# One decoder trunk, two MoE layers: first gate chunks loaded in parts, and other orders and engines for the layer norm and the routing ahead of the experts

## Chip, cores and metric

One core of a Trainium2 chip runs the whole program. The metric is the time of one execution in device microseconds; the median of three runs is given. The profile is one further execution.

## The reference

256 tokens of width 1024 go through two layers. Each layer is a mixer (HGRN2 in layer 0, differential attention in layer 1), a layer norm of `alpha * x + mix`, a mixture of 16 experts, and a layer norm of `alpha * x + ffn`. What matters here is the routing and the experts:

```python
probs = softmax(xt @ router_w); sel = probs + router_b
gscore = top_k(sel.reshape(-1, 4, 4), 2)[0].sum(-1)     # 4 groups of 4 experts
gbest = argmax(gscore)
_, idx = top_k(where(in_group(gbest), sel, -inf), 2)    # two experts of that group
gates = probs[idx] / sum(probs[idx])
h = silu(xt @ w_gate[e]) * (xt @ w_up[e]); y = (h * comb) @ w_down[e]
```

Everything is float32. The expert weights are 6 MB for each expert, 96 MB for a layer.

## The kernel before

**Projections.** The weights of the mixer come in pieces of 512 rows by 512 columns (`PIECES`, 36 in all). For each piece ScalarE writes a rounded copy (`high`), VectorE the rest (`low`), and TensorE (`piece`) makes three products: rounded weights with rounded activations, rounded weights with the rest of the activations, rest of the weights with rounded activations. Within each product it runs over two token tiles `j`. The last piece of a layer's output projection is number 19 in layer 0 and 35 in layer 1, names `(AO1, 1)` and `(BO1, 1)`. VectorE then adds the residual per token tile and takes moments (`residual_projections`): for the second column half both residuals first, then both moments.

**From the layer norm to the experts** (`layer_norm`, `route` on VectorE; `turned_sums`, `root`, `second_parts`, `normalise_for_experts` on ScalarE; `moe` on TensorE). TensorE transposes x of tile 0 and tile 1 into four PSUM banks (L1968). ScalarE copies all four to `xT` (L856), TensorE multiplies them with the router in two parts (L1978), and VectorE (tile 0, L1224) and ScalarE (tile 1, L1071) copy those out for a folding matmul (L1984). The layer norm itself is folded in later, from mean and root. VectorE aggregates the moments (L1219), adds epsilon (L1221), ScalarE takes the logarithm and the exponential of minus a half (L861, L863), VectorE sharpens the root with a Newton step (L1206 to L1208), computes the shift (L1232), and signals `ln_stat`. On that signal ScalarE starts to write the normalised x to `xn` in four quarters (L847), with the router's exponential between (L1075), and VectorE computes logits (L1505, L1510), the exponentials' sum, `sel` (L1520), then the best group: all 4 x 4 differences inside each group, compared with a margin, summed to the number of experts that beat each one (`lost`), the sum of the two that lose to at most one, the same comparisons between groups (L1527 to L1541), and the mask `both` (L1543). `step` makes VectorE wait for the instruction it has just issued. TensorE counts the ranks from `both` (L1993 to L1997), VectorE makes slots (L1551) and a pick matrix (L1457), and TensorE gathers the first pair's tokens from `xn` (L2027). In between TensorE multiplies zeros (`nothing`, L1797): 4 of 512 and 33 of 256 columns ahead of the ranks, 8 behind. Its own instructions run in order.

**Experts.** The experts run in 8 pairs (e, e + 8): gate and up (`into_hidden`, L2057), down (L2071), with adding the previous pair's outputs (L2019) and gathering for later pairs (L2038) between. A pair's weights are 12 chunks of 1 MB: `chunk_of(matrix, part, e)`. The even pairs use 12 slots of a ring, the odd pairs separate places for gate and up (`spare`, `late`, in the trace "weights" and "tail"). SyncE issues all loads in a fixed order; each is issued when TensorE has read what it overwrites (`chunk_read`). Ahead of the stage it has loaded the first pair and, except for one up chunk and parts that the ring needs, the second. Its first load within the stage overwrites gate part 0 of the first pair with that of the third; it waits for the end of that part's matmuls:

```python
load_step(layer, p, p % 2, NEXT_GATES[0:1])
sp.wait_ge(xe_ps, GATHERS * layer + 1)
sp.wait_ge(xr_ready, 2 * layer + 2)
load_chunk(layer, 1, 1, UP, 1, 0)
order = NEXT_GATES[1:] + NEXT_UPS + DOWNS
```

**GpSimd** weighs pick matrices (L760, L767) and, beside the first pairs, applies the layer norm to x in place (`affine`: L744, L748) and scales it (L777).

## Time and profile before

| | us |
|---|---|
| median of 3 runs | 709.13 (708.81 to 710.08) |
| the profiled execution | 710.35 |
| its span in the trace | 708.5 |
| TensorE busy | 692.6 (98%) |
| VectorE busy | 288.6 (41%) |
| ScalarE busy | 231.8 (33%) |
| GpSimd busy | 105.7 (15%) |

The span runs from the first to the last instruction of the trace; 1.85 us of the execution lie outside. "Busy" counts all instructions alike: for TensorE also the multiplications of zeros. The DMA moved 347 GB/s over the span, and up to 423 in single slices of it.

### The profile page before, as it was taken

Reading aid. Unit: us, or ns where it says so; the run is one execution under the profiler, and the core shown is the slowest. Engines: PE = TensorE matmul, PEld = TensorE weight load, DVE = VectorE, ACT = ScalarE, POOL = GpSimd, SP = SyncE. Lnnn points to the kernel's source line nnn. Section 1 sums busy time; section 2 is a strip of 40 time slices with the busy share of each in tenths; the row PEclk is TensorE's granted clock in tenths of the full one; section 3 lists DMA queues with packets and bytes.
Section 4 is the critical chain, followed back from the end, with each engine's and each line's share of the span. In section 5 each row is a group of like instructions: output and inputs, shape, how many; then the busy total and the mean of one; then the engine's idle time right before and its main releaser. Section 6 shows DMA issues by size and latency. Waiting matters only on the chain.

```text
span 708.5 us, 13562 instructions
## 1 busy us (share of the span) xinstructions
PE 692.6 (98%) x5542; PEld 413.0 (58%) x5543; DVE 288.6 (41%) x540; ACT 231.8 (33%) x434; POOL 105.7 (15%) x69
## 2 busy tenths in 40 slices
PE   9999999999999999999999999999999999999994
PEld 7989888864235335335379987886423533533532
DVE  5589956583011112112067676668301111211205
ACT  4466457161111112012064566626111111201202
POOL 3015100019300000000213200001930000000023
PEclk9999999999999999999999999999999999999998
DMA  8999334889999999999999743488999999999992
GB/s 319 297 385 359 141 118 179 319 334 389 420 421 422 421 423 422 422 421 422 416 386 390 268 169 119 179 315 338 386 420 420 422 422 422 422 421 422 422 420 83
DMA packets 51447, 246.16 MB, mean 347 GB/s; under 512 B 6265, under 2 KB 6610, under 8 KB 26834
## 3 DMA queue, kind: packets, MB, share of 16 engines
q1 hardware_dynamic: 51410, 245.65, 86.7%
q8 instruction: 25, 0.41, 0.2%
q14 instruction: 12, 0.10, 0.0%
HBM read 244.58 MB, written 1.05 MB: 347 GB/s over the span
## 4 chain that ended last, share of the span: by engine, by line
PE 87%; DMA 8%; DVE 1%; ACT 1%; issue 1%; SPq 0%; POOL 0%; POOLq 0%; DVEq 0%; ACTq 0%
PE ps L2057 27%; PE ps L1847 15%; PE ps L2071 14%; PE ps L1842 13%; DMA tail<-in_moe_w_up 8%; PE ps L2019 4%; PE ps L2038 3%; PE ps L1797 2%; PE ps L1775 1%; PE ps L2027 1%; PE ps L2108 1%; DMA x_sb<-in_x 1%; ACT xT L856 1%; DVE stats L1664 1%; PE ps L1882 1%
## 5 line engine op out<-in xcount | busy, mean ns | idle before, releaser
L2057 PE MATMUL ps<-weights,scratch 128*32 128x512 f32 (+1 forms) x1536 | 167.8, 592 | 0.0
L2057 PEld LDWEIGHTS ps<-weights,scratch 128*32 128x32 f32 x1536 | 50.0, 110 | 113.8 <-issue 113.8
L2071 PE MATMUL ps<-weights,scratch 128*32 128x512 f32 (+1 forms) x1024 | 113.6, 594 | 0.0
L1187 DVE TENSOR_TENSOR ring_lo<-weights,w_hi 128x2048 fp32r<-128x2048 f32 x36 | 83.1, 2326 | 14.7 <-ACT w_hi L812 14.5
L1640 DVE TENSOR_TENSOR scratch<-ps,early 128x512 f32<-128x512 f32 x16 | 11.1, 692 | 183.9 <-PE ps L2057 183.9
L812 ACT ACTIVATE w_hi<-weights 128x2048 fp32r<-128x2048 f32 x35 | 66.6, 1915 | 25.6 <-PE ps L1847 15.6
L2071 PEld LDWEIGHTS ps<-weights,scratch 128*32 128x32 f32 x1024 | 31.5, 110 | 70.3 <-issue 70.3
L1652 DVE SCALAR_TENSOR_TENSOR rounded<-ps,gslot,rounded 128x512 fp32r<-128x512 f32 x32 | 24.0, 751 | 92.1 <-ACT rounded L1057 92.1
L2057 PE MATMUL ps<-tail,scratch 128*32 128x512 f32 (+1 forms) x512 | 56.8, 592 | 2.0 <-DMA tail<-in_moe_w_up 2.0
L1057 ACT ACTIVATE rounded<-ps,gslot 128x512 fp32r<-128x512 f32 x32 | 22.0, 688 | 88.9 <-PE ps L2071 88.9
L760 POOL TENSOR_TENSOR early<-rounded,gate_of 128x256 f32<-128x256 f32 x14 | 8.6, 616 | 280.8 <-PE ps L2126 279.9
L1022 ACT ACTIVATE scratch<-ps,ln_col 128x256 f32<-128x256 f32 (+1 forms) x40 | 19.3, 540 | 89.9 <-PE ps L2038 84.6
L1040 ACT ACTIVATE early<-ps 128x512 f32<-128x512 f32 x16 | 9.6, 597 | 95.1 <-PE ps L2057 95.1
L2057 PEld LDWEIGHTS ps<-tail,scratch 128*32 128x32 f32 x512 | 16.5, 110 | 40.8 <-issue 40.8
L2019 PE MATMUL ps<-rounded,early_r 128*128 128x512 f32 x128 | 35.9, 410 | 0.0
L1842 PE MATMUL ps<-x_lo,w_hi 128*128 128x256 f32 x256 | 33.8, 285 | 0.0
L748 POOL TENSOR_TENSOR x_sb<-x_sb,scratch 128x2048 f32<-128x2048 f32 x6 | 29.5, 4919 | 26.6 <-DVE scratch L1192 26.2
L1842 PE MATMUL ps<-x_hi,ring_lo 128*128 128x256 f32 x256 | 33.4, 283 | 0.0
L1623 DVE TENSOR_SCALAR scratch<-ps,ln_col 128x256 f32<-128x256 f32 (+1 forms) x40 | 18.7, 512 | 33.4 <-PE ps L2038 33.0
L2038 PE MATMUL ps<-rounded 128*128 128x256 f32 x128 | 32.2, 290 | 0.0
L767 POOL TENSOR_TENSOR early<-rounded,gate 128x256 f32<-128x256 f32 x2 | 5.5, 2740 | 178.1 <-DVE scratch L1623 178.1
L1842 PEld LDWEIGHTS ps<-x_hi,ring_lo 128*128 128x128 f32 x256 | 31.9, 192 | 0.2 <-DVE ring_lo L1187 0.2
(278 smaller groups left out, 973.4 us busy)
## 6 DMA issues: line engine op xcount, KB each, us to landing
weights<-in_moe_w_gate SPq DMA_DIRECT2D x64, 1024.0 KB, 15.4
weights<-in_moe_w_down SPq DMA_DIRECT2D x64, 1024.0 KB, 14.0
weights<-in_moe_w_up SPq DMA_DIRECT2D x32, 1024.0 KB, 15.0
tail<-in_moe_w_up SPq DMA_DIRECT2D x32, 1024.0 KB, 20.4
weights<-in_a_w_in SPq DMA_DIRECT2D x15, 1024.0 KB, 12.8
weights<-in_kv_w SPq DMA_DIRECT2D x8, 1024.0 KB, 15.3
weights<-in_a_w_out SPq DMA_DIRECT2D x4, 1024.0 KB, 14.6
weights<-in_b_w_q SPq DMA_DIRECT2D x4, 1024.0 KB, 15.1
```

The lines of the kernel that those rows point to most:

```text
L748: last = pool.tensor_tensor(x[:, :, :], x[:, :, :], ln_gb[:, j, :].unsqueeze(1).to_broadcast([P, TT, D]), op)
L812: nc.scalar.activation(w_hi[:, i % HI, :, :].rearrange("p k n -> p (k n)"), ring[:, piece_slot(i), :, :].rearrange("p k n -> p (k n)"), AC ...
L1022: last = nc.scalar.activation(xe[:, k, cols], ps[:, bank, j * width:(j + 1) * width], ACT.Identity, scale=ln_col(2 * layer, 0, k), bias=ln ...
L1057: nc.scalar.activation(ys_hi[:, part * COLS:(part + 1) * COLS], ps[:, bank, :], ACT.Copy, scale=gslot[:, 0:1]).then_inc(ys_act, 1)
L1187: V.tensor_tensor(low_part(i), ring[:, piece_slot(i), :, :], w_hi[:, i % HI, :, :].bitcast(F32), ALU.subtract).then_inc(lo_ready, 1)
L1652: V.scalar_tensor_tensor(ys_lo[:, cols], ps[:, bank, :], gslot[:, 0:1], ys_hi[:, cols].bitcast(F32), ALU.mult, ALU.subtract).then_inc(ys_d ...
L1842: last = mm(ps[:, bank, c * T:(c + 1) * T], w[:, k, first:first + P], xs[:, HALF_K * part + k, :], start=opens and c == 0 and k == 0, stop ...
L1847: last = mm(ps[:, bank, :], xs[:, HALF_K * part + k, j * P:(j + 1) * P], w[:, k, :], start=opens and k == 0, stop=closes and k == HALF_K - ...
L2019: last = mm(ps[:, 2 * t + j, :], put[:, t * P:(t + 1) * P], part[:, j * COLS:(j + 1) * COLS], start=False, stop=True, skip_group_check=True)
L2038: last = mm(ps[:, banks[j // 2], first:first + 4 * SLOTS], part[:, t, k * P:(k + 1) * P], pick[:, t, :, :].rearrange("p e s -> p (e s)"), ...
L2057: last = mm(ps[rows, bank, :], own[:, HALF_K * part + k, rows], w, start=part == 0 and k == 0, stop=part == 1 and k == HALF_K - 1)
L2071: last = mm(ps[rows, bank, :], hT[:, 2 * part + k, rows], w, start=part == 0 and k == 0, stop=part == 1 and k == 1)
```

## The change

1. **Gate chunks in parts.** The loads that overwrite the first pair's gate part 0 are cut by rows k: k=0 and k=1 are each issued when TensorE has read that k, the last two when it has read the whole part. The short ones are counted on a semaphore `rows_in`, for which SyncE waits before the next gate part.
2. **Last piece by token tile.** TensorE makes all three products of tile 0 before those of tile 1, and waits for the low weights at the start of the piece. VectorE takes residual and moments of tile 0, then of tile 1.
3. **The fourth xT copy** goes from ScalarE to VectorE.
4. **Root.** ScalarE takes the logarithm from the aggregated variance with epsilon as its bias. VectorE halves the variance meanwhile, and has the shift before the root is sharpened; both are then finished by one operation each. This serves all four layer norms.
5. **Groups.** The best group is found by the maximum of the six pair sums of each group; the comparisons inside groups, which the mask needs, run between, with waits only where a result is used. The normalising sum `m2` is taken behind the pick matrix.
6. **A quarter of the rows.** The last of the four quarters of `xn` (tile 1, columns 512 to 1023) goes from ScalarE to GpSimd, on `ln_stat`.
7. 25 zero matmuls in place of 33 ahead of the ranks. Some semaphores are merged.

```diff
+            def load_first_gates(layer):
+                half = ins["moe_w_gate"].shape[2] // 2
+                for k, rows in enumerate((slice(0, 1), slice(1, 2), slice(2, 4))):
+                    if rows.stop < HALF_K:
+                        sp.wait_ge(gate_rows, PAIRS * layer + k + 1)
+                    else:
+                        sp.wait_ge(*chunk_read(PAIRS * layer + 1, GATE, 0))
+                    for e in range(2):
+                        c = chunk_of(GATE, 0, e)
+                        w = ins["moe_w_gate"][layer, 2 + PAIRS * e, 0:half, :].rearrange("(p k) n -> p k n", p=P)
+                        arrived = rows_in if rows.stop < HALF_K else arrive[chunk_slot(layer, c)]
+                        sp.dma_start(chunk_place(layer, 0, c)[:, rows, :], w[:, rows, :]).then_inc(arrived, 16)
...
-                        load_step(layer, p, p % 2, NEXT_GATES[0:1])
+                        load_first_gates(layer)
                         sp.wait_ge(xe_ps, GATHERS * layer + 1)
                         sp.wait_ge(xr_ready, 2 * layer + 2)
                         load_chunk(layer, 1, 1, UP, 1, 0)
+                        sp.wait_ge(rows_in, 64 * (layer + 1))
...
+                pool.wait_ge(ln_stat, 2 * layer + 1)
+                pool.tensor_scalar(xn[:, 1, COLS:D].rearrange("p (k n) -> p k n", k=HALF_K),
+                                   x[:, 1, COLS:D].rearrange("p (n k) -> p k n", k=HALF_K), mv[:, 1, 0:1], rs[:, 2, 1:2],
+                                   ALU.subtract, ALU.mult).then_inc(x_done[1], 1)
...
+            def root_of_variance(i):
+                act.wait_ge(var_ready, i + 1)
+                nc.scalar.activation(rs[:, 1, 0:TT].unsqueeze(2), mv[:, :, 1:2], ACT.Ln, bias=eps[:, 0:1]
+                                     ).then_inc(ln_step, 1)
...
-                step(last)
-                V.tensor_scalar(rs[:, 0, 0:TT].unsqueeze(2), mv[:, :, 1:2], LN_EPS, None, ALU.add).then_inc(var_ready, 1)
+                last.then_inc(var_ready, 1)
+                dve.wait_ge(var_ready, rt_call + 1)
+                step(V.tensor_scalar(rs[:, 0, 0:TT].unsqueeze(2), mv[:, :, 1:2], LN_EPS, -0.5, ALU.add, ALU.mult))
                 if i % 2 == 0:
+                    dve.wait_ge(z_ps, 4 * (i // 2) + 4)
+                    V.tensor_copy(xT[:, HALF_K:KT, P:T], ps[:, 3, :].rearrange("p (k t) -> p k t", k=HALF_K)
+                                  ).then_inc(z_dve, 1)
...
-                step(rstd(rt_call, ln_values))
-                V.scalar_tensor_tensor(rs[:, 4, 0:TT].unsqueeze(2), mv[:, :, 0:1], -1.0, rs[:, 2, 0:TT].unsqueeze(2),
-                                       ALU.mult, ALU.mult).then_inc(ln_stat, 1)
+                dve.wait_ge(root_ready, rt_call + 1)
+                for t in range(TT):
+                    V.scalar_tensor_tensor(t3[:, t:t + 1], first[:, t:t + 1], half_var[:, t:t + 1], first[:, t:t + 1],
+                                           ALU.mult, ALU.mult)
+                step(V.scalar_tensor_tensor(shift.unsqueeze(2), mv[:, :, 0:1], -1.0, first.unsqueeze(2), ALU.mult, ALU.mult))
+                V.scalar_tensor_tensor(y, t3, 1.5, first, ALU.add, ALU.mult)
+                V.scalar_tensor_tensor(shift, t3, 1.5, shift, ALU.add, ALU.mult).then_inc(ln_stat, 1)
...
+                V.tensor_tensor(two_of[:, :, 0:2], four[:, :, 0:4:2], four[:, :, 1:4:2], ALU.add)
+                sums_done = mark(V.tensor_tensor(two_of[:, :, 2:6].rearrange("p g (a b) -> p g a b", a=2), ...))
+                apart = mark(V.tensor_tensor(versus[:, :, :, :], *others(four, NG, 4), ALU.subtract))
+                dve.wait_ge(dve_step, sums_done)
+                best = mark(V.reduce_max(gs, two_of, axis=AX.X))
+                dve.wait_ge(dve_step, apart)
+                won = mark(V.tensor_tensor(versus, versus, margin, ALU.is_gt))
+                dve.wait_ge(dve_step, best)
+                step(V.tensor_tensor(of_groups, *others(gs.rearrange("p (t g) -> p t g", t=TT), TT, GROUPS), ALU.subtract))
+                ahead = mark(V.tensor_tensor(of_groups, of_groups, margin, ALU.is_gt))
+                dve.wait_ge(dve_step, won)
+                V.reduce_sum(lost.rearrange("p (g e) -> p g e", e=4), versus[:, :, :, :], axis=AX.X)
+                dve.wait_ge(dve_step, ahead)
+                step(V.reduce_sum(beaten.rearrange("p (t g) -> p t g", t=TT), of_groups, axis=AX.X))
...
+                if (n, part) in ((AO1, 1), (BO1, 1)):
+                    pe.wait_ge(lo_ready, i + 1)
+                    for j, (number, (w, xs)), k in itertools.product(range(2), enumerate(products), range(HALF_K)):
+                        last = mm(ps[:, 4 + 2 * (n % 2) + j, :], xs[:, HALF_K * part + k, j * P:(j + 1) * P], w[:, k, :],
+                                  start=False, stop=number == 2 and k == HALF_K - 1, skip_group_check=True)
...
-                for _ in range(33):
+                for _ in range(25):
                     nothing(BANK_C, COLS // 2)
...
+                            if matrix == GATE and part == 0 and k < 2 and not odd:
+                                last.then_inc(gate_rows, 1)
```

`mark` signals `dve_step` like `step` but does not wait. The margin operand is broadcast over the groups.

## Rows read from the trace of the kernel before

**Rows 1.** Waits of TensorE: us, times, longest; then a row of its timeline.
```profile
PE ps L2057 <- DMA tail<-in_moe_w_up: 2.0, 2, 1.0
...
681.22 3.21 PE L2057 MATMUL ps<-tail,scratch 128*32 x28 [1.04 <-DMA tail<-in_moe_w_up]
```

**Rows 2.** Windows: start:end, then busy us by engine, granted clock, DMA share, GB/s.
```profile
156.00:162.00 6.00, 6.00 (x60) 1.89 (x56) 5.79 (x18) 2.37 (x2) 4.85 (x2) 1.00 0.33 87
492.00:498.00 6.00, 5.99 (x58) 1.93 (x60) 5.65 (x13) 2.98 (x2) 4.25 (x2) 1.00 0.27 68
340.00:345.00 5.00, 4.04 (x44) 1.05 (x40) 0.00 (x0) 0.60 (x1) 0.00 (x0) 1.00 1.01 419
```

**Rows 3.** Timeline of SyncE: DMA issues ahead of the second pair, layer 0.
```profile
159.25 0.80 SPq L533 DMA_DIRECT2D weights<-in_moe_w_gate  x2
```

**Rows 4.** Chain of work that ended last: gate and up of the first pair.
```profile
155.55 13.94 PE ps L2057 x128
```

**Rows 5.** Timeline of TensorE in layer 0: matmuls of zeros and the gather.
```profile
145.88 4.63 PE L1797 MATMUL ps<-zeros 128*128 128x512 bf16 x37
...
151.72 3.81 PE L2027 MATMUL ps<-rounded,weights 128*128 128x128 f32 x32
```

**Rows 6.** Timeline of VectorE from the last residual to the slots, layer 0.
```profile
142.10 0.69 DVE L1254 SCALAR_TENSOR_TENSOR x_sb<-x_sb,ps 128x512 f32<-128x512 f32 x1 [0.22 <-PE ps L1847]
142.71 1.28 DVE L1258 BATCH_NORM_STATS2 stats<-x_sb 128x6 f32<-128x512 f32 x2
144.02 0.28 DVE L1219 BATCH_NORM_AGGREGATE mv<-stats 128x2 f32<-128x12 f32 x2
144.34 0.17 DVE L1221 TENSOR_SCALAR rs<-mv 128x2 f32<-128x2 f32 x1
...
145.12 0.16 DVE L1206 SCALAR_TENSOR_TENSOR rs<-rs 128x2 f32<-128x2 f32 x1 [0.21 <-ACT rs L863]
...
145.70 0.16 DVE L1232 SCALAR_TENSOR_TENSOR rs<-mv,rs 128x2 f32<-128x2 f32 x1
145.98 0.38 DVE L1505 SCALAR_TENSOR_TENSOR rt<-router_sums,rs 128x16 f32<-128x16 f32 x2
...
148.15 0.29 DVE L1527 TENSOR_TENSOR versus<-rt 128x128 f32<-128x128 f32 x1
...
150.25 0.19 DVE L1543 SCALAR_TENSOR_TENSOR both<-rt,rg 128x32 bf16<-128x32 f32 x1
...
150.92 0.19 DVE L1551 SCALAR_TENSOR_TENSOR slot<-ps,both 128x32 f32<-128x32 f32 x1
```

**Rows 7.** Timeline, layer 1: low weights, then weight loads of the last piece.
```profile
468.48 4.49 DVE L1187 TENSOR_TENSOR ring_lo<-weights,w_hi 128x2048 fp32r<-128x2048 f32 x2
...
472.86 2.23 PEld L1847 LDWEIGHTS ps<-w_hi,rounded 128*128 128x128 f32 x10
```

**Rows 8.** Timeline of ScalarE in layer 0: xT copies and the last normalisations.
```profile
142.70 2.06 ACT L856 ACTIVATE xT<-ps 128x512 f32<-128x512 f32 x4 [12.71 <-PE ps L1968]
...
147.39 3.70 ACT L847 ACTIVATE weights<-x_sb,rs 128x512 f32<-128x512 f32 x3
```

**Rows 9.** Groups by line and shape: a VectorE copy of 512 elements from PSUM.
```profile
L1192 DVE COPY scratch<-ps 128x512 f32<-128x512 f32 x4 | 2.8, 688 | 7.0 <-PE ps L1842 7.0
```

**Rows 10.** Timeline rows of GpSimd and VectorE where both work at once.
```profile
63.39 1.62 POOL L733 TENSOR_TENSOR scratch<-scratch 128x512 f32<-128x512 f32 x1
...
63.78 1.77 DVE L1338 TENSOR_TENSOR scratch<-scratch 128x512 f32<-128x512 f32 x1
...
159.88 7.56 POOL L744 TENSOR_SCALAR x_sb<-x_sb,mv,rs 128x1024 f32<-128x1024 f32 x2
...
176.86 5.38 POOL L777 TENSOR_SCALAR x_sb<-x_sb 128x2048 f32<-128x2048 f32 x1
...
160.04 1.07 DVE L1478 COPY slot_of<-slot 128x16 f32<-128x16 f32 x1
...
161.09 0.16 DVE L1480 TENSOR_TENSOR rt<-rt,rg 128x16 f32<-128x16 f32 x1
```

More of the change, by code:

```diff
@@ L851, in turned_sums @@
             def turned_sums(layer):
-                for n in range(4):
+                for n in range(3):
                     act.wait_ge(z_ps, 4 * layer + n + 1)
@@ L1079, in _ @@
             turned_sums(0)
-            root(2, ln_values)
+            root_of_variance(2)
             second_parts(0)
@@ L1084, in _ @@
             normalise_for_experts(0, 0, 1)
-            for half in range(2):
-                normalise_for_experts(0, 1, half)
+            normalise_for_experts(0, 1, 0)
             moe(0)
-            root(3, ln_values)
+            root_of_variance(3)
             normalise(1)
@@ L1168, in _ @@
             normalise_for_experts(2, 0, 1)
-            for half in range(2):
-                normalise_for_experts(2, 1, half)
+            normalise_for_experts(2, 1, 0)
             moe(1)
-            root(7, ln_values)
+            root_of_variance(7)
             normalise_last()
@@ L1270, in residual_projections @@
                     dve.wait_ge(proj_ready, 2 * n0 + 2 + t + 1)
-                    add_residual(t, 1, ps[:, 6 + t, :])
-                for t in range(TT):
-                    moments(t, 1, added[0] - 1 + t)
-            V.memset(zeros16[:, :], 0.0).then_inc(zeros_ready, 1)
+                    residual(t, 1, ps[:, 6 + t, :])
+            V.memset(zeros16[:, :], 0.0).then_inc(consts_dve, 1)
+            V.memset(eps[:, :], LN_EPS)
             dve.wait_ge(consts_ready, 1)
-            V.tensor_copy(ident_r[:, :], ident[:, :]).then_inc(ident_ready, 1)
+            V.tensor_copy(ident_r[:, :], ident[:, :]).then_inc(consts_dve, 1)
             for half, bank in enumerate((1, 3)):
@@ L1496, in te @@
                     return ap.rearrange("p (t e) -> p t e", t=TT)
-                lg, ex, sel, lost, best2, pm = (rt[:, i, :] for i in range(6))
+                lg, ex, sel, lost, _, pm = (rt[:, i, :] for i in range(6))
                 m2 = rg[:, 0, 0:TT]
@@ L1525, in route @@
                 four = sel.rearrange("p (g e) -> p g e", e=4)
-                other, this = (four.unsqueeze(axis).to_broadcast([P, NG, 4, 4]) for axis in (2, 3))
-                step(V.tensor_tensor(versus[:, :, :, :], other, this, ALU.subtract))
-                step(V.tensor_tensor(versus[:, :, :, :], versus[:, :, :, :],
-                                     margin[:, :, :].unsqueeze(1).to_broadcast([P, NG, 4, 4]), ALU.is_gt))
-                step(V.reduce_sum(lost.rearrange("p (g e) -> p g e", e=4), versus[:, :, :, :], axis=AX.X))
@@ L1531, in route @@
-                step(V.scalar_tensor_tensor(best2, lost, 1.5, sel, ALU.is_lt, ALU.mult))
-                gs = rg[:, 7, 0:NG]
-                step(V.reduce_sum(gs, best2.rearrange("p (g e) -> p g e", e=4), axis=AX.X))
-                sums = gs.rearrange("p (t g) -> p t g", t=TT)
-                other, this = (sums.unsqueeze(axis).to_broadcast([P, TT, GROUPS, GROUPS]) for axis in (2, 3))
-                step(V.tensor_tensor(versus[:, 0:TT, :, :], other, this, ALU.subtract))
-                step(V.tensor_tensor(versus[:, 0:TT, :, :], versus[:, 0:TT, :, :],
-                                     margin[:, :, :].unsqueeze(1).to_broadcast([P, TT, GROUPS, GROUPS]), ALU.is_gt))
@@ L1540, in route, with others @@
-                beaten = rg[:, 8, 0:NG]
-                step(V.reduce_sum(beaten.rearrange("p (t g) -> p t g", t=TT), versus[:, 0:TT, :, :], axis=AX.X))
+                two_of = rt[:, 6:8, :].rearrange("p a n -> p (a n)")[:, 0:6 * NG].rearrange("p (g n) -> p g n", n=6)
+                gs, beaten = rg[:, 7, 0:NG], rg[:, 8, 0:NG]
+                of_groups = rg[:, 9, :].rearrange("p (t a b) -> p t a b", t=TT, a=GROUPS)
+                def others(ap, n, size):
+                    return [ap.unsqueeze(axis).to_broadcast([P, n, size, size]) for axis in (2, 3)]
@@ L1819, in piece @@
                     pe.wait_ge(x_hi_dve, 2 * call + part + 1)
-                for number, (w, xs) in enumerate(((hi, his), (hi, los), (lo, his))):
+                products = ((hi, his), (hi, los), (lo, his))
+                if (n, part) in ((AO1, 1), (BO1, 1)):
[3 more added lines that the diff above has]
+                                  start=False, stop=number == 2 and k == HALF_K - 1, skip_group_check=True)
+                        if number == 2 and k == HALF_K - 1:
+                            last.then_inc(proj_ready, 1)
+                    return
+                for number, (w, xs) in enumerate(products):
                     if number == 1 and first_of_half:
```

50 lines of the change are left out of this document (34 added, 16 removed).

## The prediction, made before the changed kernel ran

> **What bounds the kernel now.** I read the waits first. In each of the two expert stages, TensorE, which is busy nearly all the time, stops once for a transfer, for the last pair's up weights: 2.0 us in two stops, the only ones of the whole trace for a weight transfer, 1.04 of it at 681.22 [rows 1] and 0.96 in the 5 us from 340 [rows 2]. The windows then show why the transfer is late although it was asked for long before. Through the stage the DMA moves about 420 GB/s with nothing to spare; but at the stage's beginning there is a hole. From 156 to 162 us it moves 87 GB/s, from 492 to 498 us 68 GB/s [rows 2]. Against 419 that is 6 x (1 - 87/419) = 4.75 us and 6 x (1 - 68/419) = 5.0 us of empty queue. The queue is empty because the buffers are full: its next transfer overwrites the first gate chunks, and SyncE issues it at 159.25 [rows 3], once the first pair has read all of gate part 0 (it began at 155.55, a quarter of 13.9 us [rows 4]). So DMA and TensorE are balanced, and the stream starts late by a wait on TensorE.
>
> The second thing that bounds the kernel is the stretch ahead of the experts, where TensorE is "busy" with matmuls of zeros. The timeline shows 37 of them from 145.88 to 150.51, and eight more up to the gather at 151.72 [rows 5]. The work that counts there is a chain on VectorE [rows 6]: residual (142.10), moments (142.71), variance (144.34), root, shift (145.70), logits (145.98), groups (148.15 to 150.25), slots (150.92), pick. What is cut from this chain comes off the kernel, in both layers, if the weights keep up.
>
> **The change, part by part.** Times are those of layer 0; layer 1 repeats them, 336.6 us later.
>
> *Gate chunks in parts.* Rows of k=0 are asked for after a quarter of the 3.5 us read of part 0 [rows 4], k=1 after half, the rest as before. The first request moves from 159.25 to about 156.6, 2.6 us ahead of where it stands relative to TensorE. One half MB takes 1.25 us at 420 GB/s, and a quarter of the read is 0.87 us, so the parts follow one another without a new hole. What is queued ahead of the hole ends at 156, the window's left edge, so there is room for it. I take 0.15 to 0.3 us off for shorter rows in 2 of the 96 MB, and are left with 2.3 us of lead. The transfers wanted at the end need 0.96 and 1.04; both stops go: **2.0 us**. The remaining lead is not worth anything, since TensorE has no other wait for it. SyncE issues six DMAs where it issued two, 0.4 us each [rows 3], and then waits for the four short ones to land, about 159; the next thing queued behind is gate part 1, which waits until 162 anyway. Cost nothing; without that cover, at most some tenths of the lead.
>
> *The last piece by token tile.* The same 24 matmuls; tile 0's sums close 2.7 us earlier, tile 1's at the same time. Residual, then moments of tile 0 move into VectorE's idle time; of the two moments behind 142.10 one is left, so aggregation starts at 142.10 + 0.69 + 0.03 + 0.69 + 0.03 = 143.54 in place of 144.02 [rows 6]. The transposes start when the piece ends, and tile 1's wait for the residual that ends at 142.79; both are unchanged. In layer 1 the piece must now have its low weights at its start: these are ready at 468.48 + 4.49 = 472.97, and TensorE's first load is at 472.86 [rows 7], so with 0.05 us for the signal it starts 0.16 us later: **-0.16 us** once.
>
> *Fourth xT copy to VectorE.* ScalarE's four copies end at 142.70 + 2.06 = 144.76 [rows 8]. VectorE is free at 143.82 (aggregation), does the halved variance, and copies 144.06 to 144.75, by the 0.69 us of a PSUM copy of that size [rows 9]. So the router's second half is not earlier. But ScalarE takes the logarithm at about 144.13, behind three copies and with no VectorE step before it. The root is there at 144.6.
>
> *Root and shift.* VectorE, busy with xT and then lgT until about 144.87, runs two tiny products, the shift, then two closing operations. Instructions that need no wait between them start 0.1 us apart (two aggregations in 0.28 us), those with one 0.20 apart (145.12, then four to 145.86) [rows 6]: 0.08 + 0.08 + 0.19 + 0.08 + 0.16 = 0.59, so the shift is out at 145.46 in place of 145.86. **0.40 us.** The second half's logits come at about 146.0 by the unchanged router path, just in time.
>
> *Groups.* From 148.15 to 150.25 eight operations wait each for the one before [rows 6]: 2.10 us. After: nine, two of 128 elements kept apart by others. I lay them out with start-to-start of duration less 0.08 where nothing is waited for and duration plus 0.03 where it is. Starts: sums 0 and 0.09, differences 0.20, maximum 0.41, comparison 0.53, group differences 0.74, comparison 0.965, lost 1.075, beaten 1.285, both 1.50. **0.60 us.** The sum m2 leaves the way from ranks to slots, which started at 150.92 behind it; by the matmuls around them the ranks were there some 0.1 us before, an estimate: **0.08 us**. Eight fewer zero matmuls take 8 x 256 of 10,496 columns, 0.9 of 4.63 us [rows 5], off a queue that ended at 150.51, so it ends at about 149.6, just behind the masks at 149.44: a tie, which the hold below, if it comes, turns into idle time.
>
> *A quarter of the rows on GpSimd.* ScalarE's normalisation ended at 151.09 [rows 8], and would now end by 149.6. GpSimd's part has an unseen price: by the 3.78 us of one 1024-wide operation of the same form [rows 10] it is between 1.9 and 3.8 us; taking 2.62 ns an element from the 5.38 us of 2048 with a constant, and the remaining 1.1 us as fixed, 512 elements cost 2.4. It starts at 145.6 and has until 150.5. Its own time is hidden in every case. Its cost is what it does to VectorE, on whose chain everything above was saved. At 63.78 a two-input VectorE operation of a width that takes 0.7 us (as at 142.10) took 1.77, ending 0.5 us after the GpSimd operation of 63.39 to 65.01. But at 159.88 a GpSimd operation of exactly the new form began, and only the VectorE copy at 160.04 was held, for 0.9 us; the two-input one at 161.09 ran in its usual 0.16 although GpSimd worked until 167.44 [rows 10]. So this form holds VectorE for the first 1.0 us of its run, or, if that goes with the width, for 0.5 us. It would start within 0.02 us of the first logit operation, and is likely to get in between the two, where a hold falls wholly on the chain; if it gets in later, most of the hold ends before the next two-input operation 0.7 us on. The bounds are 0 and 1.05 us per layer; I take 0.5, that of half the width.
>
> The Trainium skill speaks against this part: by its page "SBUF — State Buffer", section "Who interferes with whom", a VectorE instruction with two SBUF inputs and a GpSimd instruction that reads SBUF exclude each other, and the later one waits for the whole of the other. The rows of 63.39 agree; the row of 161.09 does not. By the page the sum would be that of rival 3 below; by the rows it is the one I give.
>
> *The other layer norms.* Between the layers the step ahead of the logarithm (0.2 us) goes and the chain behind it is about as long: **+0.2 us**. At the end VectorE has two copies to make meanwhile, and two more waits: **-0.08 us**.
>
> **Sum.** 2.0 + 0.2 - 0.16 - 0.08 = 1.96, and per layer 0.40 + 0.60 + 0.08 - 0.5 = 0.58, twice 1.16: 3.1 us. The profiled execution took 710.35 us, 1.85 outside its span of 708.5; the median of the runs is 709.13. I take the 3.1 from the median: 706.0 (the profiled time would go to 707.2).
>
> **Rivals.** (1) *No hold at all* on VectorE's two-input operations, as at 161.09: 1.96 + 2.16 = 4.1 us, 705.0. For it: only a copy was seen held. Against: the hold at 63.78. 25%. (2) *The full hold of the first 1.05 us*: 1.96 + 0.06 = 2.0, 707.1. 15%. (3) *The exclusive lock*: the second logit operation is held for all 2.4 us of GpSimd's work. For it: 63.78. Against: 161.09. Per layer 1.08 - 2.4 = -1.3, sum 1.96 - 2.64 = -0.7, 709.8, no change. 10%. (4) *Slower*: the same lock with GpSimd's operation at the upper price, 3.8 us, since it reads with a stride of four; per layer -2.7, sum -3.4, 712.5. It decides from a hold of 2.06 us per layer, and is beyond 0.2% from 2.8. 5%. (5) *The hole is not filled*, because the short rows move slowly or the wait for them blocks SyncE: the stops stay, 3.1 - 2.0 = 1.1, 708.0. 8%. My forecast, a hold of 0.25 to 0.8 us: 34%, by itself 705.3 to 706.6.
>
> The range takes in the forecast and rivals 1, 2 and 5 with 0.6 us for the spread of the runs: 704.4 to 708.3. What a measurement of this kernel can tell from no change is 0.2%, 1.4 us. Faster by more: forecast, 1, 2, and part of 5: 0.78. Within: 3, most of 5: 0.15. Slower: 4 and what I have not thought of: 0.07.
>
> **What the profile after would show.** Right: no wait of TensorE for the up weights; more than 200 GB/s in the six microseconds behind the first gate matmul; the groups in 1.5 us; the gather at about 151.2 in layer 0. A logit or maximum operation of 0.6 us or more beside GpSimd's start shows the hold. Wrong: a VectorE operation of 2 us there (rivals 3, 4); a wait for a transfer that stays (5); or a lower clock of TensorE, which idles up to 0.6 us before the ranks; the stop of 0.96 us left it at 1.00 [rows 2], so I price that at nothing.

## Result: 0.25% slower at first, no different the second time

| | median | lowest to highest | runs |
|---|---|---|---|
| before | 708.83 us | 708.54 to 710.15 | 20 |
| changed kernel | 711.0 us | 707.67 to 713.77 | 20 |

The ratio is 1.0025, 95% interval 1.0013 to 1.0037. Three us faster was forecast. What stands out is the spread: the kernel before repeats itself within some tenths but for single runs near 710.1, the changed one's times are spread over 6 us. Its profiled execution took 713.31 us (span 711.4), the one of before 710.35 (708.5). Both are executions with a slow beginning: at 7.4 us two matmuls of 512 columns took TensorE 1.97 us, where the profiles of experiments e1, e8 and e11 below have 1.07, and from there on everything stands 1.6 to 1.8 us later (tile 1's residual at 142.10 and 142.13, in e8 at 140.28). The two can be compared with each other, but their totals cannot be compared with those of the other profiles. Why the beginning is slow in some executions is open; the rows of the granted clock say 1.00 there in all of them.

The chain of work that ended last in the changed kernel, from the experts of layer 0 to those of layer 1 (start, length, what):

```profile
154.71 13.94 PE ps L2114 x128
...
315.50 1.91 SPq L535
317.45 26.05 DMA tail<-in_moe_w_up
343.74 3.64 PE ps L2114 x32
...
361.21 1.08 PE ps L1842 x19
362.29 2.87 issue
365.15 4.08 PE ps L1842 x41
369.23 1.75 PE ps L1820 x16
```

Cut both kernels at the same marks and compare. Up to the experts: 154.71 against 155.55 [rows 4], 0.84 us saved. From there to the transposes of layer 1's input: 369.23 - 154.71 = 214.52 against 365.42 - 155.55 = 209.87, **4.65 lost**. To the experts of layer 1 (494.90 against 492.15): 125.67 against 126.73, 1.06 saved. To the end: 216.50 against 216.35. Sum +2.9, the difference of the spans. What was changed ahead of the experts gained a little in both layers. The loss lies in the stretch from the experts to the next layer's input, at its end, where only the root of the layer norm was changed.

Two of TensorE's waits in the changed kernel (what for: us in total, times, longest):

```profile
PE ps L1842 <- issue: 2.9, 1, 2.9
PE ps L2114 <- DMA tail<-in_moe_w_up: 2.1, 2, 1.0
```

The first is new: after 19 of the 60 matmuls of zeros that keep TensorE busy between the layers it stops for 2.87 us, and no engine, semaphore or transfer of the program is what it waits for. The second is the wait that was to go, unchanged [rows 1]. VectorE had its part ready meanwhile (start, length):

```profile
363.80 1.53 DVE L1283 TENSOR_SCALAR x_sb<-ps,mv,rs 128x512 f32<-128x512 f32 x2
```

This operation began at 364.56 in the kernel before, and the transposes 0.86 us behind it. Here they could have begun at 364.66 and began at 369.23. The windows (start and end, length, busy time of TensorE, its weight loads, VectorE, ScalarE and GpSimd, then the granted clock, the DMA's share and GB/s) say why it is more than 2.87:

```profile
156.00:162.00 6.00, 6.00 (x60) 1.89 (x56) 5.90 (x17) 1.68 (x3) 5.44 (x2) 1.00 0.74 216
492.00:498.00 6.00, 5.99 (x58) 3.74 (x61) 5.55 (x22) 4.59 (x6) 1.21 (x1) 1.00 0.76 300
...
366.00:367.00 1.00, 1.00 (x12) 1.00 (x10) 0.00 (x0) 0.00 (x0) 0.00 (x0) 0.50 1.07 391
367.00:369.00 2.00, 2.00 (x23) 2.00 (x21) 0.00 (x0) 0.00 (x0) 0.00 (x0) 0.54 1.08 391
369.00:372.00 3.00, 3.00 (x32) 2.93 (x29) 1.85 (x4) 2.07 (x5) 0.00 (x0) 1.00 1.03 382
```

Behind the stop TensorE runs at 0.50 of its clock (1.2 of 2.4 GHz) for most of 3 us: 41 matmuls of zeros took 4.08 us, where the second profile of the same kernel (e11 below) has 41 of them in 2.45 at clock 1.00. That is another 1.6 us. The first two rows answer to [rows 2]: more is moved in the hole of the stream than before (216 for 87 GB/s, 300 for 68).

The routing went nearly as foreseen. VectorE and GpSimd, layer 0:

```profile
142.13 0.69 DVE L1291 SCALAR_TENSOR_TENSOR x_sb<-x_sb,ps 128x512 f32<-128x512 f32 x1 [1.31 <-PE ps L1869]
...
145.43 0.15 DVE L1268 SCALAR_TENSOR_TENSOR rs<-rs 128x2 f32<-128x2 f32 x1
145.70 0.38 DVE L1541 SCALAR_TENSOR_TENSOR rt<-router_sums,rs 128x16 f32<-128x16 f32 x2
...
146.75 0.36 DVE L1550 TENSOR_TENSOR rt<-rt,rg 128x32 f32<-128x32 f32 x1
...
148.04 0.18 DVE L1569 TENSOR_TENSOR rt<-rt 128x16 f32<-128x16 f32 x1
...
149.51 0.19 DVE L1588 SCALAR_TENSOR_TENSOR both<-rt,rg 128x32 bf16<-128x32 f32 x1
```

```profile
145.69 2.69 POOL L791 TENSOR_SCALAR weights<-x_sb,mv,rs 128x512 f32<-128x512 f32 x1 [66.62 <-DVE rs L1268]
```

From the residual to the end of the shift it is 145.58 - 142.13 = 3.45 us, 0.31 less than the 3.76 before (0.40 forecast). The groups take 149.51 - 148.04 = 1.47 us (1.50 forecast, 2.10 before), GpSimd's quarter 2.69 (2.4 forecast), and beside it VectorE loses 0.17 us, at L1550, which takes 0.36 us here and 0.19 in e1.

### The profile page after: what moved, and what is told of

Its sections match the earlier page's. It is cut to its first block, busy times and chain, and to the rows that moved or that the text cites. A ratio compares the mean times of both kernels' runs of the same rounds, so it can differ in the third digit from the quotient of the medians.

```text
span 711.4 us, 13551 instructions
## 1 busy us (share of the span) xinstructions
PE 692.4 (97%) x5526; PEld 413.2 (58%) x5527; DVE 289.6 (41%) x549; ACT 228.9 (32%) x430; POOL 110.8 (16%) x71
## 3 DMA queue, kind: packets, MB, share of 16 engines
HBM read 244.58 MB, written 1.05 MB: 345 GB/s over the span
## 4 chain that ended last, share of the span: by engine, by line
PE 86%; DMA 8%; DVE 3%; issue 1%; ACT 1%; SPq 1%; POOL 0%; POOLq 0%; DVEq 0%; ACTq 0%
PE ps L2114 27%; PE ps L2130 14%; PE ps L1901 13%; PE ps L1896 13%; DMA tail<-in_moe_w_up 7%; PE ps L2076 4%; PE ps L2095 3%; PE ps L1869 2%; PE ps L1820 1%; PE ps L1842 1%; PE ps L2084 1%; PE ps L2167 1%; DMA x_sb<-in_x 1%; PE ps L1936 1%; SPq L535 1%
## 5 line engine op out<-in xcount | busy, mean ns | idle before, releaser
L1896 PEld LDWEIGHTS ps<-x_lo,w_hi 128*128 128x128 f32 x256 | 31.8, 192 | 0.1
```

Source lines behind the costliest of these rows:

```text
L1896: last = mm(ps[:, bank, c * T:(c + 1) * T], w[:, k, first:first + P], xs[:, HALF_K * part + k, :], start=opens and c == 0 and k == 0, stop ...
```

## Experiments

All were timed in five rounds beside the kernel before (medians 708.85, 708.84 and 708.74 in the three batches, e1 to e4, e5 to e8 and e9 to e12; a single execution of it in the second took 1818.73 us and says nothing of the kernels). The interval in brackets is that of the ratio; differences of some tenths of a us between two runs are within the noise.

| run | what it is | median (lowest to highest) | ratio to before |
|---|---|---|---|
| e1 | changed kernel, 15 long matmuls of zeros for 60 short | 708.21 (706.78 to 710.19) | 0.9986 [0.9975, 0.9996] |
| e2 | changed kernel, 20 more instructions of filler ahead | 708.76 (707.61 to 710.49) | 0.9997 [0.9989, 1.0006] |
| e3 | before with the parts alone | 708.94 (707.93 to 710.92) | 1.0003 [0.9994, 1.0012] |
| e4 | changed kernel without the parts | 709.13 (708.20 to 713.72) | 1.0011 [0.9997, 1.0025] |
| e5 | e1 without GpSimd's quarter | 707.20 (706.81 to 708.16) | 0.9976 [0.9968, 0.9985] |
| e6 | e1 without the parts | 708.05 (707.29 to 709.21) | 0.9990 [0.9982, 0.9999] |
| e7 | e1 without both | 707.24 (707.00 to 708.00) | 0.9976 [0.9966, 0.9986] |
| e8 | before with 25 fillers for 33 | 709.89 (709.39 to 712.84) | 1.0021 [1.0013, 1.0030] |
| e9 | e7 with 1 MB less to load per layer | 704.81 (704.33 to 705.27) | 0.9943 [0.9930, 0.9955] |
| e10 | e6, GpSimd starts later | 708.09 (707.72 to 708.64) | 0.9989 [0.9980, 0.9997] |
| e11 | changed kernel again | 709.30 (707.97 to 712.11) | 1.0007 [0.9994, 1.0019] |
| e12 | e7 with the old groups | 708.28 (707.93 to 708.93) | 0.9991 [0.9982, 1.0000] |

### The stop between the layers

**e1: fewer, longer zeros.**

```diff
-            for _ in range(60):
-                nothing(BANK_A, COLS // 4)
+            for _ in range(15):
+                nothing(BANK_A)
```

> The changed kernel, but the 60 multiplications of zeros by 128 columns behind layer 0's experts are 15 by 512 columns: the same columns in a quarter of the instructions, so nothing is left out. Theory A (TensorE ran out of fetched instructions: it stopped for 2.87 us after 19 of the 60, for nothing the profile shows, and the clock fell): the next fetched block begins a fixed number of instructions behind the branch, so the 15 longer ones are all inside and TensorE works until the first transposes; the stop shrinks below 1 us, the granted clock stays at 1.00, and the time falls by about 3.5 us against the changed kernel's 711.0, to 707.0 to 708, with runs close together. Rival B (TensorE is held by something else at that moment, such as the transfers or the layer norm): the stop and the fall of the clock stay, 710 to 712.

708.21 us, 2.8 below the changed kernel's first median and 1.1 below its second (e11), and a little above the 707 to 708 that were expected. The same columns in a quarter of the instructions; the stop is not in the trace and the clock stays at 1.00.

**e2: the zeros 40 instructions later** (20 of the 25 fillers cut in two, each a matmul with its weight load).

```diff
-                for _ in range(25):
+                for _ in range(40):
+                    nothing(BANK_C, COLS // 4)
+                for _ in range(5):
                     nothing(BANK_C, COLS // 2)
```

> The changed kernel, but 20 of the 25 multiplications of zeros ahead of the ranks are cut in two (256 columns into twice 128): same columns and same work, but 20 more matmuls in TensorE's program ahead of the experts, in each layer. Theory A (blocks of fetched instructions end at fixed places of the program): the end of the block moves to before the branch over the overflow code, the next block is asked for while the last sums run, as in the kernel before, and the stop at the layer's end is gone: 707.0 to 708. Rival B (the place in the program is of no matter): the stop stays at 2 to 3 us and the time at 710 to 712.

In the profile the 60 short zeros run through, and no execution is above 710.5. But the median, 708.76, misses the 707 to 708 that were expected and is not clearly apart from the 709.30 of e11, so it is not shown that this edit takes the stop out of every execution. With e1 it points to the place or the number of instructions, not to what they compute.

**e8: nothing but the place, in the kernel before.**

```diff
-                for _ in range(33):
+                for _ in range(25):
                     nothing(BANK_C, COLS // 2)
```

> The kernel before with one edit: 25 filler matmuls for 33 while the routing runs, which puts TensorE's jump over the overflow and the 60 zero matmuls behind it where the changed kernel has them in the program. Nothing of the change itself is in it. Theory (the stop of 2.9 us at layer 0's end comes from the place of the jump and of the zeros among TensorE's instructions): the stop appears in this kernel too, after some 19 of the 60 zeros, in a part of the executions; the profile shows it by chance, the times show it: a spread up to 712 or 713 us and a median of 709.5 to 711. Rival (the stop comes from what else is new in the changed kernel: its requests for weights, GpSimd's or VectorE's operations): median 708.85 as before, none above 710.7. By itself the edit leaves TensorE idle for about 1.1 us more ahead of the ranks in each layer, in the shadow of VectorE.

This decides where the loss comes from. TensorE's timeline of e8 (start, length, then idle time before it and what ended it):

```profile
360.06 1.29 PE L1797 MATMUL ps<-zeros 128*128 128x128 bf16 x20
362.56 2.41 PE L1797 MATMUL ps<-zeros 128*128 128x128 bf16 x40 [1.21 <-issue]
```

The kernel before, with 16 instructions fewer ahead of the zeros (eight matmuls, eight weight loads) and no other edit, stops after 20 of its zeros (19 in the changed kernel), and its lowest time, 709.39 (median 709.89), is above the median of the unedited one. The fillers taken out leave TensorE idle for 0.9 us ahead of the ranks in each layer, but that costs nothing: from the experts of layer 0 (153.73) to the transposes (364.80) e8 takes 211.07 us, before 209.87, and that 1.20 is the stop; from there to the experts of layer 1 it is 126.67 against 126.73. No part of the change's own work is needed for the loss.

What is it? The transfers' view has queues of the kind "instruction", and on one of them, q8, a block comes just there (packets, MB, share of the engines). A tenth of a microsecond of that view in the kernel before (358.2 to 358.3 us):

```profile
q8 instruction: 1, 0.02, 65.9%
```

in the changed kernel (362.5 to 362.6):

```profile
q8 instruction: 1, 0.02, 69.1%
```

and in e8 (360.1 to 360.2):

```profile
q8 instruction: 1, 0.02, 69.4%
```

The changed kernel resumes at 365.15, e8 at 362.56, a second profile of the changed kernel (e11) at 361.69 with its block at 359.0: always 2.4 to 2.7 us behind. In the kernel before the block comes at 358.2, 3.6 us ahead of the first zero (361.83), and is in time. The view does not say whose instructions q8 brings; the timing says TensorE's, and that TensorE had run out of them.

e1's profile does not test this. Its block came at 254 us, long before it was needed, and so did e2's, at 302: there could be no stop in them with any filler. e7 below, which has e1's long zeros too, does test it. Its block (359.1 to 359.2) came as e11's did, 0.1 to 0.2 us ahead of the first zero:

```profile
q8 instruction: 1, 0.02, 69.6%
```

```profile
359.22 3.41 PE L1839 MATMUL ps<-zeros 128*128 128x512 bf16 x15
```

The 15 long zeros run through until 362.63, longer than e11 had to wait for its block. The 60 short ones of e11 stopped at 360.45, after 38 instructions. e5, e6, e10 and e12, all with the long zeros, had their blocks between 359.4 and 361.9 and show no stop either.

The Trainium skill, page "Runtime: NRT & Kernel Launch", section "Instruction fetch mechanics", says that an engine's instructions are fetched in blocks of 16 KiB, 256 instructions, by the sequencer over its own queue while the block before runs, and that a taken branch to a target outside of what is loaded forces a fetch and a stall. Ahead of the zeros TensorE jumps over the code for overflowing experts; the rows agree with the page in that the stop comes soon behind a jump and goes with a 0.02 MB block. But the stop is not at the target: it is 19 matmuls, 38 instructions, behind it.

**e11: the changed kernel again.**

> The changed kernel itself, unedited, beside the others on this chip. Theory (a stop of 1 to 3 us at layer 0's end in a part of its executions, and up to 2 us more while TensorE's clock is down): times from 707.7 to 713.8 again, median 709.5 to 711.5; a profiled execution over 710.5 us shows the stop among the 60 zero matmuls, one under 709 us does not. Rival (the first twenty executions were an accident of that chip): median 708.2 to 708.8, none over 711.

709.30 us: the wide spread is there again, the median lower, just under the range that was expected. The expectation's second half was wrong: the profiled execution took 709.0 us and has the stop, but of 1.24 us and at full clock:

```profile
359.21 1.24 PE L1842 MATMUL ps<-zeros 128*128 128x128 bf16 x19
361.69 2.45 PE L1842 MATMUL ps<-zeros 128*128 128x128 bf16 x41 [1.24 <-issue]
```

So the stop has a length that changes from run to run, at least 1.2 to 2.9 us, and can bring the halved clock on top. In other executions it is absent: e4 below has the same instructions on TensorE, its profile shows 60 zeros in one piece, and its block came at 254 us (e3's at 303), long before it was needed. What makes the sequencer ask early in one execution and behind the jump in another was not found out.

### The gate chunks in parts

**e3: the parts alone**, in the kernel before (`load_first_gates`, the marks of TensorE and the wait of SyncE, as in the diff above).

> The kernel before with the first gate chunks in parts and nothing else. My prediction's step: both waits for the last up weights go (2.0 us), 706.8. Rival C (the parts fill the hole, but the last of the 16 DMA engines is not ahead by it, as the changed kernel's waits of 1.05 us say): the wait shrinks by 0.5 us or less in each layer, 707.9 to 708.9. TensorE's program is the same length as before, so by theory A no stop at the layer's end.

No gain: 708.94, where the prediction's step would give 706.8, and TensorE's two stops for the up weights 2.5 us in total, not none.

**e4: all but the parts.**

```diff
-                        load_first_gates(layer)
+                        load_step(layer, p, p % 2, NEXT_GATES[0:1])
...
-                        sp.wait_ge(rows_in, 64 * (layer + 1))
```

> The changed kernel with the first gate chunks loaded whole again. By rival C it is the same as the changed kernel in its waits for the up weights (0.9 to 1.8 us each, since the stream starts later relative to TensorE only by what the parts gave); by my prediction's step each wait is about 1 us as before. TensorE's program is as long as in the changed kernel, so by theory A the stop at the layer's end stays, with a spread of several us among the runs: 710 to 712.

The median, 709.13, lies below the 710 to 712 expected. But two executions of twelve were at 711.8 and 713.7, as the changed kernel's, so the parts are not what makes it slow. For their worth the comparison is too loose; e5 to e7 leave the stop out.

**e5, e6, e7: with and without the parts, with and without GpSimd's quarter**, all with e1's long zeros. Without parts is the edit of e4. Without the quarter:

```diff
-                pool.wait_ge(ln_stat, 2 * layer + 1)
-                pool.tensor_scalar(xn[:, 1, COLS:D]..., x[:, 1, COLS:D]..., mv[:, 1, 0:1], rs[:, 2, 1:2],
-                                   ALU.subtract, ALU.mult).then_inc(x_done[1], 1)
...
-            normalise_for_experts(0, 1, 0)
+            for half in range(2):
+                normalise_for_experts(0, 1, half)
```

> The 15 long zero matmuls of e1_long_zeros, and ScalarE again normalises all four quarters (GpSimd's operation of 2.6 us is out). Theory (GpSimd's operation holds VectorE's first logit operation, by 0.2 us in some executions and by 1.0 in others, and both land on the chain to the ranks): TensorE's wait for `both` of 1.7 us over two layers is gone from its waits, the first logit pair takes 0.38 us, the experts of layer 0 start near 153.2 us and those of layer 1 near 489.0 in an execution that starts as e1's did, and the median lies 0.5 to 1.5 us under e1's 708.21: 706.7 to 707.7. ScalarE's fourth quarter ends about 1.2 us later than its third and would then end within 0.2 us of the first gather. Rival (what the hold takes is given back by the stream of weights, since the experts' stage ends when its last piece lands): the experts start earlier, TensorE's stops for up weights grow by as much, and the median stays at 708.2.

> The 15 long zero matmuls of e1_long_zeros, and the first gate chunks come whole, as in the kernel before. Theory (the parts are worth nothing, and spread the landings of one chunk over its 16 DMA engines): the median is that of e1, 708.2, within 0.4 us, the times lie closer together than e1's 706.8 to 710.2 and the changed kernel's, and TensorE's stops for up weights are 2.0 us in total. Rival (the parts do save a stop of 1.0 us and the lost time was all in the stop at layer 0's end): this kernel is 0.8 to 1.2 us slower than e1, 709.0 to 709.4.

> The changed kernel with its first gate chunks whole, without GpSimd's quarter and with 15 long zero matmuls for the 60 short ones: what is left of the change is the routing (last piece by token tile, the root on the side, groups by pair sums). Theory (these three parts of it cost what they bring or more): 706.8 to 707.6 us, the lowest of all so far, with the times within 1 us of each other but for late starts. Rival (the parts save a stop of 1 us): 0.8 us slower than the same kernel with parts, e5. Rival (no shortening of the routing reaches the end): 708.2 or more, as e6.

The parts cost 0.16 us with the quarter (e1 over e6) and bring 0.04 without (e5 under e7): nothing that can be told from zero, against 2.0 forecast. Why is seen in microsecond windows of the hole. Whole chunks (e7):

```profile
155.00:156.00 1.00, 1.00 (x16) 0.40 (x12) 1.00 (x1) 0.66 (x1) 1.00 (x1) 1.00 0.01 4
...
157.00:158.00 1.00, 1.00 (x12) 0.27 (x8) 0.97 (x3) 0.00 (x0) 1.00 (x2) 1.00 0.28 49
...
159.00:160.00 1.00, 1.00 (x16) 0.27 (x8) 0.97 (x6) 0.03 (x1) 1.00 (x1) 1.00 1.00 426
160.00:161.00 1.00, 1.00 (x12) 0.27 (x8) 0.12 (x1) 0.56 (x1) 1.00 (x2) 1.00 1.01 426
```

Parts (e5, whose experts begin 0.4 us later):

```profile
155.00:156.00 1.00, 1.00 (x16) 0.40 (x12) 1.00 (x1) 1.00 (x1) 1.00 (x1) 1.00 0.39 141
...
157.00:158.00 1.00, 1.00 (x13) 0.27 (x9) 0.97 (x4) 0.00 (x0) 1.00 (x2) 1.00 0.76 147
...
159.00:160.00 1.00, 1.00 (x16) 0.27 (x8) 0.93 (x9) 0.00 (x0) 1.00 (x1) 1.00 1.07 336
160.00:161.00 1.00, 1.00 (x12) 0.27 (x8) 0.55 (x1) 0.60 (x1) 1.00 (x1) 1.00 0.97 350
```

Read the last two columns together. The parts do move bytes in the hole, but at 147 GB/s the DMA engines are already 0.76 busy, and from 159 us, where the whole chunks run at 426 GB/s, the parts and what follows run at 336 and 350 with the engines full. The transfers of the nine microseconds 155 to 164, in e7 and then in e5:

```profile
DMA packets 333, 2.45 MB, mean 273 GB/s; under 512 B 33, under 2 KB 33, under 8 KB 34
...
q1 hardware_dynamic: 333, 2.45, 67.5%
```

```profile
DMA packets 920, 2.53 MB, mean 281 GB/s; under 512 B 98, under 2 KB 98, under 8 KB 869
...
q1 hardware_dynamic: 920, 2.53, 85.6%
```

A whole chunk goes in packets of 8 KB, four rows of a partition in one piece; a part breaks them up into 2 and 4 KB, and 869 of 920 packets are under 8 KB (98 of them under 512 B). For nearly the same bytes the engines are busy 85.6% instead of 67.5%. The hole is filled with slower work. When it closes, e5 has moved 0.08 MB more; with the 0.43 us by which its experts began later (153.26 for 152.83), 0.18 MB at 420 GB/s, the stream is 0.26 MB or 0.6 us ahead of where it stands beside TensorE in e7. 2.3 us were forecast, and about 1.0 is needed. TensorE's stops for the up weights are 1.6 us in e5's profile and 2.0 in e7's, but they vary from profile to profile: with parts 2.1 (changed kernel), 0.9 (e1), 2.1 (e2), 2.5 (e3) and 1.8 (e11), without parts 2.0 to 2.3. In the medians nothing shows. Why a lead of 0.6 us takes no more off the stops is not shown. The Trainium skill's rule, page "DMA: Bandwidth & Descriptors", section "Bandwidth", is to move at least 1 MiB in one DMA. It agrees with these rows in direction: the parts are 256 and 512 KB.

**e9: a real lead for the stream.** Of e7's two first gate chunks only half of the rows is loaded.

```diff
-                        load_step(layer, p, p % 2, NEXT_GATES[0:1])
+                        sp.wait_ge(*chunk_read(PAIRS * layer + 1, GATE, 0))
+                        for e in range(2):
+                            ...
+                            sp.dma_start(chunk_place(layer, 0, c)[:, 0:2, :], w[:, 0:2, :]
+                                         ).then_inc(arrive[chunk_slot(layer, c)], 16)
```

> e7_long_zeros_no_parts_no_quarter, and of the two first gate chunks of the second pair only half of the rows is loaded (the other half is the old content, so the output is not the reference's): 1 MB less of the stream of weights per layer, 2.6 us of it at 386 GB/s, at the place where the parts filled the hole with 0.7 MB. Theory A (the prediction's price: TensorE's stops for up weights go if the stream is ahead by more than 1.0 us, and are 2.0 us of the time): the last up chunk's flight is 24.7 us for 27.3, no stop for up weights is left, and the median is that of e7 less 1.6 to 2.0 us: 705.2 to 705.7. Then the parts' 0.7 MB failed because it did not reach the last of the 16 DMA engines. Theory B (a chunk lands some 28 us after its release whatever was moved earlier): flight and stops as in e7, 707.2 us.

704.81 us, 2.43 under e7 and under the 705.2 to 705.7 expected. TensorE's waits in its profile name no weights any more; the longest left is one of 1.05 us for "issue" in layer 0's mixer, at 80.6 us, which the kernel before has too (1.06 at 82.6). So the price of the two stops was right, if anything low, and a lead of the stream does take them away. The parts failed because they gave no lead.

### The routing and GpSimd

GpSimd's quarter costs 1.01 us with the parts (e1 over e5) and 0.81 without (e6 over e7). It takes them from VectorE, by a different amount from time to time. In e1 GpSimd starts 0.01 us ahead of VectorE's first logit operation:

```profile
144.12 1.33 DVE L1541 SCALAR_TENSOR_TENSOR rt<-router_sums,rs 128x16 f32<-128x16 f32 x2
```

```profile
144.11 2.63 POOL L791 TENSOR_SCALAR weights<-x_sb,mv,rs 128x512 f32<-128x512 f32 x1 [66.64 <-DVE rs L1268]
```

and the pair takes 1.33 us for 0.38, a hold of 0.95. In e6 the two start in the same order and as close together:

```profile
143.93 0.38 DVE L1540 SCALAR_TENSOR_TENSOR rt<-router_sums,rs 128x16 f32<-128x16 f32 x2
```

```profile
143.92 2.70 POOL L790 TENSOR_SCALAR weights<-x_sb,mv,rs 128x512 f32<-128x512 f32 x1 [66.62 <-DVE rs L1267]
```

and the pair takes its usual 0.38; 0.18 us is lost at a later operation, as in the changed kernel's first profile. Both cases come in one execution: e4 and e11 lose 0.2 us in layer 0 and 0.95 in layer 1. What decides between them was not found out; it is neither the operation nor the order to 0.01 us.

**e10: GpSimd starts when the logits stand.**

```diff
-                pool.wait_ge(ln_stat, 2 * layer + 1)
+                pool.wait_ge(logit_ready, layer + 1)
                 pool.tensor_scalar(xn[:, 1, COLS:D]...
```

> e6_long_zeros_no_parts with one edit: GpSimd starts its quarter when the logits stand (the semaphore that also starts ScalarE's exponential), about 1.4 us later, so it cannot start beside VectorE's first logit operation. Theory (the long hold of 1.0 us falls on the VectorE operation that starts together with GpSimd's, and later ones lose 0.2 us): the hold moves to the operation after the maximum; if it is 0.2 us each time the median is 707.4 to 707.6, between e7's 707.24 and e6's 708.05, and its times lie close together; if it is 1.0 us wherever two operations start together, the median stays at 708.0. GpSimd's quarter ends near 149.8 us in after's time, 1.1 us ahead of the gather's start. Rival (GpSimd's operation now ends too late and holds the gather): 708.2 or more, with a wait of TensorE for GpSimd in the trace.

The hold moved to the operation that takes the pair of `sel`, with 0.64 in both layers, between the two sizes that the expectation names; no wait for GpSimd appeared. VectorE and GpSimd of e10:

```profile
145.45 1.02 DVE L1555 SCALAR_TENSOR_TENSOR rt<-router_bias,rg,rt 128x16 f32<-128x16 f32 x2
146.51 0.18 DVE L1568 TENSOR_TENSOR rt<-rt 128x16 f32<-128x16 f32 x1
```

```profile
145.04 2.58 POOL L790 TENSOR_SCALAR weights<-x_sb,mv,rs 128x512 f32<-128x512 f32 x1 [67.98 <-DVE rt L1549]
```

L1555 takes 1.02 us for 0.38; all that VectorE does afterwards, from 146.51 on, runs in its usual time although GpSimd works until 147.62. The times now lie within 0.9 us, but the median is as good as e6's, 708.09 for 708.05: neither of the two starts tried is free.

**e12: the old groups in e7** (the block of the diff above put back).

> e7_long_zeros_no_parts_no_quarter with the groups compared as in the kernel before (no pair sums, every step waited for). Theory (the groups' 0.60 us per layer reach the end in full): e7's 707.24 plus 1.2 us, 708.2 to 708.6. Rival (the stream of weights sets the stage's end, so an earlier start of the experts comes back as a stop): within 0.3 us of e7.

1.04 us over e7, of 1.2, and within the range expected: the shorter groups reach the end nearly in full.

## Why the prediction was wrong

**The step that failed most: the parts, 2.0 us.** "The parts follow one another without a new hole", with 0.15 to 0.3 us off for shorter rows, had the full rate of 420 GB/s for 256 KB requests. They ran at 107 to 154 in the hole and at 336 to 350 behind it, in packets that keep the engines busy without the bytes (e5 against e7). Rival 5 had this case, at 8%; it is what happened, and its 708.0 is what the kernel does without the new stop (708.21 in e1, 708.05 in e6). That the two stops are worth 2.0 us on the end was right (e9: 2.4). Two small sums were off and change nothing in this: a hold of 0.25 us gives 705.5, not 705.3, and rival 5 with 0.6 us of spread reaches 708.6, outside the stated 708.3.

**What was in no case: TensorE's instructions.** The eight fillers taken out were priced as columns, and the jump and the zeros behind them not looked at. The new place of what follows them made TensorE wait 1.2 to 2.9 us, for an instruction block by all that the rows show; e8 has the same stop with this edit alone. The clock was named as a way to be wrong, but for the idle time ahead of the ranks, where it stayed at 1.00 even with 0.9 us of idle time (e1); it fell behind the stop of 2.87 us.

**The routing: right, sizes a little off.** Without parts and stop (e6) the sum was 3.1 - 2.0 = 1.1 us; measured 708.84 - 708.05 = 0.79. Without GpSimd's part as well (e7) it was 2.1; measured 1.60. Of the missing 0.5, 0.4 is a wait that the terms did not have: with all four quarters on ScalarE the gather waits 0.2 us per layer for the last one. By its parts: groups 1.2, measured 1.04 (e12); root and shift 0.40 per layer, 0.31 in the trace; GpSimd's quarter 0.5 per layer, measured 0.4 to 0.5 in the medians. That is luck in part: it is what the hold takes less the 0.2 us for which the gather would otherwise wait, so by the medians the hold itself is 0.6 to 0.7, an estimate from the same differences. It is made of holds of 0.2 and of 0.95 us, close to rival 1's and rival 2's cases by turns; the layer norm between the layers +0.2, in the trace nothing, 363.80 - 362.12 = 1.68 us from aggregation to the last operation for 364.56 - 362.90 = 1.66.

**The exclusive lock** (rivals 3 and 4) did not come. The Trainium skill, page "SBUF — State Buffer", section "Who interferes with whom", would have VectorE's two-input operation wait for all of GpSimd's 2.6 us; the longest hold by this operation in any of these traces is 0.95 us, and two-input operations ran freely during the rest.

**Together:** 3.1 forecast; 2.0 never came, and the stop with what it does to the clock takes 1.1 us (e11 over e1) to 2.8 (the first twenty over e1, not timed together). The best version is e7 or e5, 707.2 us, 0.24% below the kernel before: the shorter routing (in e5 with the parts, which add nothing), GpSimd left out, and the zeros between the layers in 15 matmuls.

## What to carry to other kernels

A request cut into parts is worth its lead only if its packets stay long: look at the busy share and the GB/s of the hole together, since engines that are 0.76 busy at 147 GB/s have little left to gain. Every instruction taken out or put in moves all that follow it in the engine's program, and in e8 sixteen of them brought a stop elsewhere; where an engine races through many short instructions soon behind a jump, look for "issue" in its waits and for the instruction queue among the transfers, and use few long instructions as filler. And when a kernel's times spread that did not before, look at single executions before the median is explained.

## What the runs showed of the hardware

TensorE stopped for 1.2 to 2.9 us where an instruction block came late; in three profiles 2.4 to 2.7 us pass from the block's transfer to the next matmul, and the stop of 2.87 us was followed by some 3 us at half the clock. A GpSimd tensor_scalar of 128x512 takes 2.58 to 2.70 us in the rows above, and holds VectorE only in its first 1.5 us: for 0.17 or 0.95 us beside the same operations with the same start, and for 0.64 us when it starts later. Loads cut into packets of 2 and 4 KB kept the DMA engines 0.76 busy at 147 GB/s, and full at 336 to 350 GB/s where packets of 8 KB reached 426.
